# Sums of w_ada on two engines, memory turns between mixer blocks, a late norm factor, and a new order in the second block's attention

## What is computed

```
# first block
mod = silu(c) @ w_ada + b_ada                    # 1024 -> 6 x 1024: sh1, sc1, g1, sh2, sc2, g2
h = standardize(x) * (1 + sc1) + sh1
mix = hybrid_mixer(h)                            # mLSTM heads and an S5 scan, gated, @ w_mix_out
x = layer_norm(ALPHA * x + (1 + g1) * mix)
h = standardize(x) * (1 + sc2) + sh2
x = layer_norm(ALPHA * x + (1 + g2) * conv_glu_ffn(h))
# second block
y = rmsnorm(x, norm_mix_g) @ w_in_2              # q, k, v (512 each), conv value a, conv gate g
q, k = partial_rotary(q), partial_rotary(k)
att = dilated_sliding_attention(q, k, v)         # 8 heads of 64
conv = silu(layernorm(dwconv31(a * sigmoid(g)) + b))
x = x + concat(att, conv) @ w_out
xk, xv = rmsnorm(mem) @ w_xk, rmsnorm(mem) @ w_xv    # 256 memory rows
x = x + cross_attention(rmsnorm(x), xk, xv) @ w_xo
x = x + square(relu(rmsnorm(x) @ w_up)) @ w_down     # then a last rmsnorm
```

## Time and profile before

| | |
|---|---|
| median of three runs | 1710.02 us |
| profiled execution, whole / span | 1708.97 / 1707.2 us |
| TensorE busy | 1593.7 us (93%) |
| VectorE, ScalarE, POOL busy | 771.1, 618.0, 621.3 us |
| mean granted TensorE clock | 0.981 |

### The profile page before, as it was taken

How to read it: one execution, slowest core, us unless ns; L and a number is a source line. 1 busy time by engine, 2 the same in 40 slices (tenths; PEclk the granted TensorE clock), 3 DMA queues, 4 the chain that set the end, 5 groups by cost and what they waited for, 6 DMA issues and landing times.

```text
span 1707.2 us, 18472 instructions
## 1 busy us (share of the span) xinstructions
PE 1593.7 (93%) x7476; PEld 1291.2 (76%) x7476; DVE 771.1 (45%) x1343; ACT 618.0 (36%) x893; POOL 621.3 (36%) x266
## 2 busy tenths in 40 slices
PE   1899999999698999999999899899999999999998
PEld 1688867778577788878887787677886788888886
DVE  7899233646737344123308699462432531012203
ACT  3443554442315433123322423474343343123312
POOL 0453223234235344434444453102322344434442
PEclk9999999999899999999999999899999999999999
DMA  9294432159423445233332432001221233233332
GB/s 310 81 150 119 112 93 74 50 157 303 156 86 111 124 136 155 93 87 98 94 118 81 135 99 87 25 1 49 74 75 50 86 101 105 91 90 96 104 94 74
DMA packets 221605, 180.26 MB, mean 106 GB/s; under 512 B 24136, under 2 KB 184264, under 8 KB 221392
## 3 DMA queue, kind: packets, MB, share of 16 engines
q1 hardware_dynamic: 212304, 166.48, 33.7%
q10 hardware_dynamic: 9216, 12.60, 2.4%
HBM read 172.49 MB, written 6.55 MB: 105 GB/s over the span
## 4 chain that ended last, share of the span: by engine, by line
PE 78%; DVE 14%; ACT 4%; issue 1%; DMA 1%; POOL 1%; ACTq 0%; SPq 0%; DVEq 0%
PE bank L617 15%; PE bank L618 14%; PE bank L619 14%; PE bank L655 7%; PE bank L657 7%; PE bank L656 7%; DVE bank L2085 5%; PE bank L693 3%; DVE grow L1683 1%; PE bank L951 1%; PE bank L981 1%; PE bank L863 1%; POOL w_lo L2250 1%; PE bank L1038 1%; ACT scr L1131 1%
## 5 line engine op out<-in xcount | busy, mean ns | idle before, releaser
L2250 POOL TENSOR_TENSOR w_lo<-raw,w_hi 128x1024 fp32r<-128x1024 f32 (+1 forms) x246 | 598.5, 2436 | 992.6 <-ACT w_hi L1105 992.5
L1105 ACT ACTIVATE w_hi<-raw 128x1024 fp32r<-128x1024 f32 (+1 forms) x246 | 257.8, 1050 | 374.4 <-PE bank L657 294.4
L617 PE MATMUL bank<-h_hi,w_hi 128*128 128x512 f32 x968 | 381.6, 394 | 7.1 <-DVE h_lo L1575 2.6
L619 PE MATMUL bank<-h_hi,w_lo 128*128 128x512 f32 x968 | 378.4, 391 | 0.0
L618 PE MATMUL bank<-h_lo,w_hi 128*128 128x512 f32 x968 | 378.1, 391 | 0.0
L617 PEld LDWEIGHTS bank<-h_hi,w_hi 128*128 128x128 f32 x968 | 182.6, 189 | 51.3 <-DVE h_lo L1575 5.6
L619 PEld LDWEIGHTS bank<-h_hi,w_lo 128*128 128x128 f32 x968 | 182.4, 188 | 38.3
L618 PEld LDWEIGHTS bank<-h_lo,w_hi 128*128 128x128 f32 x968 | 182.5, 189 | 37.8 <-issue 0.7
L2085 DVE SCALAR_TENSOR_TENSOR bank<-att_area,cols,bank 128x512 f32<-128x512 f32 x116 | 87.6, 756 | 4.0
L657 PE MATMUL bank<-w_hi,u_lo 128*128 128x512 f32 x224 | 88.6, 396 | 0.0
L656 PE MATMUL bank<-w_lo,u_hi 128*128 128x512 f32 x224 | 88.6, 395 | 0.0
(11 more groups left out here) (408 smaller groups left out, 2600.5 us busy)
## 6 DMA issues: line engine op xcount, KB each, us to landing
raw<-in_w_in SPq DMA_DIRECT2D x57, 512.0 KB, 4.1
raw<-in_w_ffn_up SPq DMA_DIRECT2D x44, 512.0 KB, 3.8
raw<-in_w_up SPq DMA_DIRECT2D x32, 512.0 KB, 4.0
raw<-in_w_down SPq DMA_DIRECT2D x32, 512.0 KB, 3.7
ada_ring<-in_w_ada SPq DMA_DIRECT2D x24, 512.0 KB, 5.7
raw<-in_w_ffn_down SPq DMA_DIRECT2D x20, 512.0 KB, 3.7
raw<-in_w_s_glu SPq DMA_DIRECT2D x16, 256.0 KB, 3.1
raw<-in_w_mlstm_down SPq DMA_DIRECT2D x8, 512.0 KB, 6.6
```

The costliest lines, as they stand in the source:

```text
L617: te.matmul(ps, wv[0][:, i, :], rh, start=(i == 0), stop=False)
L619: last = te.matmul(ps, wv[1][:, i, :], rh, start=False, stop=(i == kt - 1))
L1105: sc.activation(W_HI[SLOT[key]][:, 0:n], raw[:, RAW_SLOT[key], 0:n], ACT.Copy).then_inc(*hi_set.up(key))
L2250: gp_.tensor_tensor(W_LO[s_][:, 0:n], raw[:, RAW_SLOT[key], 0:n], W_HI[s_][:, 0:n].bitcast(F32), ALU.subtract).then_inc(*lo_made.up(key))
```

## The change

- Start: w_ada's first two parts come in eight DMAs of 1 MB. VectorE adds pieces 0 to 4 and 6 of part 0 and 0 to 6 of part 1 (into a second buffer, `scr`); TensorE multiplies pieces 5 and 7, and 7, by silu(c) itself and then adds VectorE's sum in the same bank. Some turns go between. The modulation is done in place in PSUM, even tiles by ScalarE and odd ones by VectorE, and a turn's bank is freed by the low part. `us` 0 and 1 are computed tile by tile together (`feature_pair`); the old function of that name is now `feature_halves`.
- POOL makes the low parts of `us` 0 to 3 before its memset of `toep`.
- Memory: squares and scaling on ScalarE, at `ya` 4 and 5; the turns, two tiles to a bank, between the first blocks of `mix`; the w_ada steps of `ya` 6 are done after `ya` 7's output.
- h2: modulation as at the start, `fg` 0 and `fv` 0 as a pair.
- Second block: the stream is turned without its norm, half of it before the last `xv` block and half inside the first pair of conv blocks. The norm's factor of each row is applied afterwards: for q, k, v as the scale of the copy out of PSUM, for the conv blocks by two VectorE products with a tile whose every row holds the 512 factors, made by four products of ones with diagonals.
- Taps: 11 instead of 13 behind each conv block, rotation 0 after 28 more, rotation 1 after 12, then 25, 9 behind the first maxima, 3 instead of 10 behind a head. The exps of head 0 go ahead of the copies of v. The turn of output tile 3 goes behind the second `out` block.
- Several semaphores are merged into shared ones.

```diff
+        ada_place = [(0, 2 * i, part(buf, 2 * (i % 2) * D, 2, D)) for i, buf in enumerate((flat_xc, flat_xc, flat_xm, flat_xm))]
+        ADA_PE = ((5, 7), (7,))
+        ada_acc = [grow, scr[:, 0:2, :].rearrange("p a b -> p (a b)")]
...
+        def first_columns(part_):
+            ps = take("misc", ("ada", part_), mod_set[part_])
+            pe.wait_ge(*c_set.all)
+            for kk in ADA_PE[part_]:
+                n = 4 * part_ + kk // 2
+                pe.wait_ge(*ada_in[n].all)
+                for f in range(KD):
+                    te.matmul(ps[:, f:f + 1], ada_place[n][2][:, kk % 2, f * P:(f + 1) * P], c_act[:, kk:kk + 1], start=(kk == ADA_PE[part_][0] and f == 0), stop=False)
...
-            columns(0)
-            columns(1)
-            pe.wait_ge(*xn_set["x3"])
-            for f in range(KD):
-                transpose(("h1", f), [xn1[:, t, f * P:(f + 1) * P] for t in range(TT)], h1_sv[f])
+            first_columns(0)
+            other_columns(0)
+            for f in range(3):
+                turn_h1(f)
+            first_columns(1)
+            turn_h1(3)
+            other_columns(1)
+            for f in range(4, 7):
+                turn_h1(f)
+            turn["misc"] = 7
+            turn_h1(7)
...
+            feature_pair([("us", 0), ("us", 1)], h_hi, h_lo, h1_ready, [us_out[0], us_out[1]])
...
-            pe.wait_ge(*mem_norm.all)
-            for f in range(KD):
-                transpose(("mn", f), [mem_tok[:, t, f * P:(f + 1) * P] for t in range(MT)], mn_ls[f])
...
                 token(("mix", c, g), KD, y_hi, y_lo, y_ready, None, range(4 * c, 4 * c + 4))
+                if c == 0:
+                    pe.wait_ge(*mem_norm.all)
+                    for f in range(4 * n, 4 * n + 4, 2):
+                        transpose(("mn", f // 2), [mem_tok[:, t, f_ * P:(f_ + 1) * P] for f_ in (f, f + 1) for t in range(MT)], mn_ls[f + 1])
...
+                    if (c, g) == (1, KD - 2):
+                        turn_stream(0, 4)
...
+            feature_halves([("cg", 0), ("cv", 0)], h_hi, h_lo, h3_ready, [cg_lin[0], u_mul[0]], lambda: turn_stream(4, KD))
...
+            ps = take("misc", "r_row", r_row_out[0])
+            for t in range(TT):
+                pe.wait_ge(*r_diag_set[t])
+                last = te.matmul(ps[:, t * P:(t + 1) * P], ones[:, :], r_diag[:, t, :], start=True, stop=True)
...
+        def modulated(stage, f, scale, bias, sv_sig, dv_sig, hi_sig):
+            ps = ps_of((stage, f))[:, :]
+            if f % 2 == 0:
+                act.wait_ge(*turned[stage, f])
+                sc.activation(ps, ps, ACT.Identity, bias=bias, scale=scale).then_inc(*sv_sig.up(f))
+                act.wait_ge(*sv_sig[f])
+            else:
+                act.wait_ge(*dv_sig[f])
+            sc.activation(h_hi[:, f, :], ps, ACT.Copy).then_inc(*hi_sig.up(f))
...
+        def modulated_low(stage, f, scale, bias, dv_sig, hi_sig, lo_sig):
+            dve.wait_ge(*turned[stage, f + 1])
+            ps = ps_of((stage, f + 1))[:, :]
+            ve.tensor_scalar(ps, ps, mod[:, scale + f + 1:scale + f + 2], mod[:, bias + f + 1:bias + f + 2], ALU.mult, ALU.add).then_inc(*dv_sig.up(f + 1))
+            for f_ in (f, f + 1):
+                low_part(hi_sig, f_, h_lo[:, f_, :], ps_of((stage, f_))[:, :], 1.0, h_hi[:, f_, :], lo_sig)
...
             for m in range(AT):
+                gate, val = ps_of(("cg", m))[:, :], ps_of(("cv", m))[:, :]
...
+                ve.tensor_tensor(scr[:, m % NSCR, :], gate, r_row, ALU.mult).then_inc(*cg_lin.up(m))
+                dve.wait_ge(*gemm["cv", m])
+                ve.tensor_tensor(val, val, r_row, ALU.mult).then_inc(*cv_lin.up(m))
...
-                some_taps(13)
+                some_taps(11)
```

More of the change, by code:

```diff
@@ L162, in signal, with stages, products @@
             return Signal(sem(name), order, by)
-        def stages(name, **orders):
+        def stages(name, by=1, **orders):
             keys = {stage: range(order) if isinstance(order, int) else order for stage, order in orders.items()}
-            whole = signal(name, [(stage, key) for stage in keys for key in keys[stage]])
+            whole = signal(name, [(stage, key) for stage in keys for key in keys[stage]], by)
             return [Stage(whole, stage) for stage in keys]
+        def products(name, *kinds):
+            whole = signal(name)
+            return [Stage(whole, kind) for kind in kinds]
         te, sc, ve, gp_, sy = nc.tensor, nc.scalar, nc.vector, nc.gpsimd, nc.sync
@@ L626, in feature, with feature_halves @@
             product(key, ps[:, 0:n], wv, KD, hi, lo, ready)
-        def feature_pair(keys, hi, lo, ready, frees, between):
+        def feature_halves(keys, hi, lo, ready, frees, between):
             made = []
@@ L640, in feature_pair @@
                 product(key, ps[:, :], wv, KD, hi, lo, ready, KD // 2)
+        def feature_pair(keys, hi, lo, ready, frees):
+            made = []
+            for key, free in zip(keys, frees):
+                ps = take("acc", key, free)
+                (wv,) = block(key)
+                made.append((key, ps, wv))
+            for i in range(KD):
+                rh, rl = at(hi, lo, i)
+                pe.wait_ge(*ready[i])
+                for key, ps, wv in made:
+                    te.matmul(ps[:, :], wv[0][:, i, :], rh, start=(i == 0), stop=False)
+                    te.matmul(ps[:, :], wv[0][:, i, :], rl, start=False, stop=False)
+                    last = te.matmul(ps[:, :], wv[1][:, i, :], rh, start=False, stop=(i == KD - 1))
+                    if i == KD - 1:
+                        last.then_inc(*gemm.up(key))
         def token(key, kt, hi, lo, ready, free, banks=(0, 1, 2, 3)):
@@ L694, in transpose, with other_columns @@
             last.then_inc(*turned.up(key))
+        def first_columns(part_):
[6 more added lines that the diff above has]
+                    te.matmul(ps[:, f:f + 1], ada_place[n][2][:, kk % 2, f * P:(f + 1) * P], c_act[:, kk:kk + 1], start=(kk == ADA_PE[part_][0] and f == 0), stop=False)
+        def other_columns(part_):
+            pe.wait_ge(*ada_sum[part_])
+            for f in range(KD):
+                last = te.matmul(bank[bank_at["ada", part_]][:, f:f + 1], ada_acc[part_][:, f * P:(f + 1) * P], ones[:, 0:1], start=False, stop=(f == KD - 1))
+            last.then_inc(*ada_col.up(part_))
         def columns(part_):
@@ L711, in tensor @@
             pe.wait_ge(*s5_in.all)
+            ring["misc"], turn["misc"] = [4, 5, 6, 1, 2, 3, 0, 7], 7
             for i in range(2):
@@ L1673, in add_gated, with ada_dve @@
                 dve.settle().bn_stats(stats[:, 2 * t + c, :], z).then_inc(*dve.step())
+        def ada_dve(p_):
+            return [kk for kk in range(KD) if kk not in ADA_PE[p_]]
         def ada_add(p_, kk, wv, mark):
@@ L2027, in vector @@
                 inner_norm(f"m{at_ // 2}n", at_, LN_EPS, False)
-            for f in range(KD):
-                low_part(h2_hi, f, h_lo[:, f, :], scr[:, f % NSCR, :], 1.0, h_hi[:, f, :], h2_lo)
+            dve.wait_ge(*mod_set[4])
+            for f in range(0, KD, 2):
+                modulated_low("h2", f, 3 * KD, 2 * KD, h2_dv, h2_hi, h2_lo)
             for k_ in range(2):
@@ L2109, in vector @@
             dve.wait_ge(*band_in.all)
-            for c in range(3):
-                for g in range(0, KD, 2):
-                    if c > 0 and g == 0:
-                        some_taps(2)
-                        rotate(c - 1)
-                    elif c < 2:
-                        some_taps(7)
+            some_taps(28)
+            rotate(0)
+            some_taps(12)
+            rotate(1)
+            some_taps(25)
             def maxima(h):
@@ L2131, in vector @@
             maxima(0)
+            some_taps(9)
             for h in range(H2):
```

217 lines of the change are left out of this document (124 added, 93 removed).

## The result

The changed kernel took 1668.2 us (median of four executions, 1663.67 to 1669.49), the kernel before 1708.55 beside it: ratio 0.9757, 95% interval 0.974 to 0.9775. Four more executions of the same kernel later (experiment "again") gave 1664.2; the pooled median of the eight is 1666.8, and the experiments are held against that. The forecast was 1660, a gain of 50 us; measured are 41.

A forecast was written before the change was run, and what follows sets the result against it. TensorE was taken as the bound, busy 1593.7 of 1707.2 us, leaving 113 us of idle to win back. The terms summed to 50.1 us, taking 1708.97 to 1658.9, forecast as a 1660 median; range 1648 to 1678.

The forecast's parts named there:

- Start: Kernel start up to the first blocks: faster modulation and paired blocks gain 6.3 us net (4.3 to 8.3).
- the charge of 2 for POOL: At the start, 2 us taken off the 8.3 us gain for TensorE waiting on POOL's low parts.
- A gain made ahead of such a stretch is carried to the end: Gapless TensorE stretches between the changed stages: earlier gains pass through whole, since TensorE's own blocks start the helpers; change 0.
- Mixer: Memory turns placed between mixer blocks remove a 16.95 us delay and a slow clock; gain 16.5 us (10 to 17.5).
- h2: h2 and first FFN pair: shorter turn chain, mostly offset by the pair ending together; gain 0.5 us (0 to 4).
- Late norm: Second block's stream and conv blocks: norm factor applied afterwards removes waits and slow clock; gain 11 us (7 to 13).
- rival D: New VectorE instructions are held behind POOL's running low parts, making the kernel slower, 1721 us; chance 0.05 with similar outcomes.
- Rotation and exps: Second block's attention: earlier rotation 1 and exps, less a 1.6 us fourth-score wait; gain 6.5 us (0 to 8).
- Heads and out: Fewer taps behind heads and full-clock turns gain 7.8 us; moving the last output turn gains 1.5.
- B: Rival: starts bound elsewhere, by slow POOL low parts and late w_ada steps; mixer gives 9, total 1671; chance 0.15.
- A: Rival: VectorE becomes the bound from the conv to the heads; total 1674; chance 0.15.
- C: Rival: stalls merely move to the next block and only the mixer gain stays; about 1692; chance 0.05.

The follow-up runs named there:

- fill_start: Changed kernel plus nine matmuls without a reader in TensorE's idle ahead of the eighth turn at the start; 1662.16 us.
- small_order: Changed kernel with three instructions moved in their queues: POOL's toep memset earlier, ScalarE's last om high part before its DMA issues, its root earlier; 1660.63 us.
- late_start: Changed kernel plus 22 single-column products without a reader ahead of the second column product, delaying the start by 10.04 us; 1669.3 us.
- taps: Changed kernel with 20 conv taps instead of 25 ahead of the first maxima and 11 instead of 9 behind them; 1660.43 us.
- exps_after: Changed kernel with the exps of head 0 put back behind ScalarE's copies of v; 1673.2 us.
- mem_front: Changed kernel with all four memory turns put back ahead of the first mixer block; 1676.95 us.
- together_front: together plus 64 turns without a reader in the first DMA wait and six added matmuls ahead of two turns of the mixer heads; 1649.1 us.
- fill_later: Changed kernel plus matmuls without a reader ahead of five later TensorE waits (186, 241, 508, 528, 721 us); 1660.06 us.
- turns_behind: Changed kernel, late norm factor kept, with all eight stream turns put back behind the last xv block; 1662.43 us.
- together: Changed kernel plus fill_start, fill_later without its 186 us place, small_order and taps; 1647.5 us.

## Why the forecast was right in direction and 9 us too far

The mixer and the heads came as forecast. The miss is made of four things: a low clock charged at nothing at the start, waits and low stretches between 84 and 371 us that the sum took as fixed, two terms of the late norm, and the wait at the fourth score. How large it came out is partly chance: 9.2 us in the first trace, 6.6 in the second.

**Start, 6.3 against 4.95.** The 8.3 us gross were right; the charge of 2 for POOL was too high (1.09 + 0.21 measured). The step that failed is "a 10 us idle left the granted clock at 1.00, so I charge nothing": the spacing shows half speed for the eleven first matmuls, 2.2 us, and fill_start gets 2.7 back. The trace of before had the evidence, in a row that I did not weigh:

```profile
51.37 4.27 PE L693 MATMUL bank<-ident,s5a 128*128 128x128 f32 x24
```

That is 0.178 us a turn, where 16 at full clock take 1.92, 0.12 each. The rule of the Trainium skill that I had set aside (TensorE: Matmul & The Clock Gate, What's actually happening) is that the clock is held back by default and released by activity. The spacing agrees with it, 0.43 us against 0.228. The Trainium skill (TensorE: Matmul & The Clock Gate, Seeing it yourself) also warns that the trace's clock events can be unreliable on trn2, which this stretch bears out.

**"A gain made ahead of such a stretch is carried to the end"**, 0 against -4.35 (and -1.94). From 560 us on it held. From 84 to 371 us the first trace lost 0.8 us at the wait at 186 us, 1.62 to a low stretch behind it, 0.3 at the wait at 241 and 1.67 to the longer low stretch there, 4.4 in all; "again" lost 0.06, 0.44 and 1.54 (a low stretch at 358 us; before, one of 1.65 came just behind the event that closes this stage). The first of these is the time of ScalarE's eight DMA issues, which varies between executions; small_order takes the wait away. The low stretches follow idles, but by chance: in the traces of the changed kernel, again and late_start 13 of the 16 idles of 1.9 us or more behind the start were followed by one, 2 of the 6 of about 1.5 us in the mixer's heads, and no shorter one. Even that is no rule (the stretch at 1120 us in taps). My sum counted low stretches where waits were removed and forgot that each wait that stays can draw one.

**Mixer, 16.5 against 17.2**: right by its mechanism. TensorE's first output matmul starts at 448.48 right behind the last input one, and no wait for mn_lo is left in either trace, only one of 1.84 us in the trace of exps_after. mem_front shows the wait where it was forecast.

**h2, 0.5 against -0.1** (-0.4 in "again"): no gain is there, a miss of less than 1 us.

**Late norm, 11 against 8.55.** Two mis-sized terms. First, the low clock: "about 2" behind the waits and 2.1 in the turns ("3.8 instead of 5.9") make 4.1, where the trace of before has 1.71 + 1.68 = 3.4, and the 1.68 is the turns themselves. Second, "written near 938, before TensorE asks": less what had been gained by then this is 920, but it was 926.7. The root stood behind a high part on ScalarE (3.33 us), and two additions to sums of 128x2 elements took 2.18 and 2.25 us instead of 0.16, each as long as a low part of POOL was running. That is the mechanism of rival D at a place I had not looked at (the kernel before has such additions too, of up to 2.3 us); it cost 1.23 us of TensorE, 3.92 in the trace of exps_after. The products with a PSUM operand were never held: L1779 took 0.82, L2207 and L2209 0.69 us. The Trainium skill (SBUF — State Buffer, Who interferes with whom) has it that two SBUF inputs contend with POOL's reads and one does not. Both findings fit that. The stage then adds up: waits removed 7.7 (5.48 + 2.25), low clock 3.4, new waits 1.23 + 0.72, products 0.9, which is 8.3 against the 8.55 measured.

**Rotation and exps, 6.5 against 4.62.** The 3.2 us of the rotation came, with 1.5 of low clock, and the exps' 4.9 came. The wait at the fourth score was 3.39 instead of 1.6: VectorE needed 102.3 us from the factor row (forecast 101.7), TensorE came 0.4 earlier, and I had let the wait end at the start of the maximum instead of at its end, 0.75 later. With the low stretch behind it (1.71) it took the exps' gain back whole. Two changed numbers of taps got 5.3 us back.

**Heads and out, 9.3 against 10.1**: right. The waits of 3.68 and 1.50 us are gone, and with them low stretches of 2.10 and 2.38.

**The rivals.** The whole time, 1668.2 us (pooled 1666.8), lies at the upper edge of the forecast's own range and nearer to B's 1671 than to my 1660, but not by B's mechanism: B had the mixer at 9 (17.2 measured). Its waits for low parts were there, 1.09 + 0.21 us at the start and 1.95 at 186, and small_order removed them by the order of the queues, though the low parts at the start still took 3.5 us each. A is out (taps). C is out, since the stage gains stand in the table. D is true only for some tiny operations.

## What to carry to other kernels

Measure TensorE's clock by the distance of starts. Price every idle of about 2 us or more of TensorE at its length and, in most executions (13 of 16 here), a further 1.6 us. If it can't be removed, matmuls without a reader in a free bank, no longer than the wait, mostly keep the clock (4 to 7 us for five places here; at one place in together_front they did not). Before calling a difference of a few us the work of a change, compare the same stretch with a second trace of the same kernel. After moving work in front of a maximum, a root or an eviction, ask which single instruction TensorE's next bank hangs on, and count to its end, not its start.

## What was not expected of the hardware

- Half speed with a granted clock of 1.00: 0.43 us between matmuls at 53 to 57 us. In fill_later, taps, turns_behind and together the column falls to 0.50 at 41 us and agrees with the spacing from there, but ahead of that it reads 1.00 in them too, while twelve turns at 34 to 35 us take 2.80 us, 0.233 each.
- Eight DMA issues on ScalarE's queue took 7.24 to 8.58 us in nine executions, and a wait of TensorE followed them one for one.
- The whole trace of small_order reads a granted clock of 0.95, yet from 560 to 700 us TensorE started as many matmuls as the changed kernel at 1.00:

```profile
560.00:700.00 140.00, 140.00 (x610) 114.13 (x609) 46.82 (x70) 41.66 (x52) 61.21 (x26) 0.95 0.41 125
```

- A single-column matmul takes 0.218 us at the low and 0.113 at the full clock (together_front), so it does not take the same time at either, as theory 2 there had it.
